# Row sums of the modulation slabs as a high and a low part, the low part by GpSimd

## What is computed

```python
for l in range(DEPTH):
    mod = (silu(c) @ ada_w[l] + ada_b[l])            # 6144 values a layer
    sh1, sc1, g1, sh2, sc2, g2 = split(mod, 6)
    hx = modulate(rms_norm(x, norm_mix_w[l]), sh1, sc1)
    ...
    xq, xdq, xg = split(hx @ w_in[:, :QG_W])         # layer 0: the input projection
    xk, xv, xdk, xdv = split(hx @ w_in[:, QG_W:])    # also of the context rows hc
```

## Time and profile before

| | |
|---|---|
| median of 3 runs | 1220.41 us (1220.31 to 1221.9) |
| the profiled execution | 1222.1 us, of which the span is 1220.2 us |
| PE busy | 1039.8 us (85%) |
| DVE busy | 935.0 us (77%) |
| ACT busy | 605.2 us (50%) |
| POOL busy | 166.7 us (14%) |

### The profile page before, as it was taken

One profiled execution on the slowest core, in us unless ns is written; L12 is line 12 of the kernel. 1 busy time (PEld: TensorE's weight loads), 2 busy tenths in 40 slices (PEclk: granted clock), 3 DMA queues, 4 the chain that ended last, 5 costly groups with the idle time before them and its releaser, 6 DMA issues. The chain is left out here.

```text
span 1220.2 us, 13889 instructions
## 1 busy us (share of the span) xinstructions
PE 1039.8 (85%) x4830; PEld 802.0 (66%) x4830; DVE 935.0 (77%) x1042; ACT 605.2 (50%) x614; POOL 166.7 (14%) x172
## 2 busy tenths in 40 slices
PE   6789999997898983999999999239579999999970
PEld 1576767774565452788888888138558888888860
DVE  5578888964993337799999998273569999999955
ACT  1534222222663122777777776023347777777731
POOL 0100200000100004410000000221063211221005
PEclk9899999997999985999999999659579999999995
DMA  9625798555014024999999997494179999999936
GB/s 372 241 69 211 257 326 311 206 207 224 10 60 129 35 100 136 292 411 413 415 413 414 413 414 312 145 352 140 52 227 392 413 414 415 413 414 414 413 128 229
DMA packets 142861, 334.14 MB, mean 274 GB/s; under 512 B 10848, under 2 KB 12840, under 8 KB 142688
## 3 DMA queue, kind: packets, MB, share of 16 engines
q1 hardware_dynamic: 122936, 279.69, 60.5%
q10 hardware_dynamic: 12392, 28.68, 6.3%
q0 software_dynamic: 7488, 25.19, 5.4%
HBM read 310.42 MB, written 23.15 MB: 273 GB/s over the span
## 5 line engine op out<-in xcount | busy, mean ns | idle before, releaser
L1828 DVE TENSOR_TENSOR w_lo<-ring,w_hi 128x2048 fp32r<-128x2048 f32 x192 | 431.3, 2285 | 25.4 <-ACT w_hi L1674 22.1
L1674 ACT CAST w_hi<-ring 128x2048 fp32r<-128x2048 f32 x192 | 365.8, 1914 | 131.6 <-DMA ring<-in_moe_w_up 50.2
L1919 PE MATMUL bank<-w_hi,xT_hi 128*128 128x512 f32 x512 | 205.2, 401 | 8.1 <-DVE xT_lo L1835 8.1
L1919 PE MATMUL bank<-w_hi,xT_lo 128*128 128x512 f32 x512 | 201.5, 394 | 0.0
L1919 PE MATMUL bank<-w_lo,xT_hi 128*128 128x512 f32 x512 | 201.1, 393 | 0.0
L1368 PE MATMUL bank<-ring_last_parts,arena_parts 128*128 128x512 f32 (+1 forms) x320 | 117.7, 398 | 5.4 <-DVE ring_parts L988 2.7
L1919 PEld LDWEIGHTS bank<-w_hi,xT_hi 128*128 128x128 f32 x512 | 97.3, 190 | 29.4 <-DVE xT_lo L1835 9.8
L1919 PEld LDWEIGHTS bank<-w_hi,xT_lo 128*128 128x128 f32 x512 | 97.1, 190 | 21.2
L1919 PEld LDWEIGHTS bank<-w_lo,xT_hi 128*128 128x128 f32 x512 | 97.5, 190 | 19.4
L1046 DVE SCALAR_TENSOR_TENSOR gate_b<-ring,silu_c,gate_b 128x512 f32<-128x512 f32 x140 | 105.9, 756 | 4.5
L1934 PE MATMUL bank<-w_hi,hT_hi 128*128 128x512 f32 x256 | 101.2, 395 | 7.5 <-DVE w_lo L1828 7.5
(11 more groups left out here) (246 smaller groups left out, 1425.5 us busy)
## 6 DMA issues: line engine op xcount, KB each, us to landing
ring<-in_moe_w_gate SPq DMA_DIRECT2D x64, 1024.0 KB, 11.5
ring<-in_moe_w_up SPq DMA_DIRECT2D x64, 1024.0 KB, 13.4
ring<-in_moe_w_down SPq DMA_DIRECT2D x64, 1024.0 KB, 11.1
ring<-in_ada_w SPq DMA_DIRECT2D x21, 2048.0 KB, 8.7
y_scratch<-shared ACTq DMA_DIRECT2D x32, 512.0 KB, 6.0
ring<-in_w_in ACTq DMA_DIRECT2D x21, 512.0 KB, 3.8
shared<-in_ada_w SPq DMA_DIRECT2D x2, 2048.0 KB, 16.0
x_res<-in_x SPq DMA_DIRECT2D x8, 512.0 KB, 12.4
```

What stands on the lines that cost most here:

```text
L1674: nc.scalar.copy(w_hi[:, buf(u, p), :], half(raw(e, p))).then_inc(s_hi, 3 if isinstance(e, int) and (e, p) == (-1, 3) else 1)
L1828: V.tensor_tensor(w_lo[:, buf(u, p), :], half(raw(e, p)), w_hi[:, buf(u, p), :].bitcast(F32), ALU.subtract).then_inc(s_lo, 3 if isinstance ...
L1919: last = pe.matmul(bank[:, b, :], xs[:, kk, :], ws[:, k, :], start=(kk == 0 and i == 0), stop=(kk == KD - 1 and i == 2))
```

## The change

The sum over partitions of the 18 slabs inside the projection is made from two fp32r parts. ScalarE casts `ada_acc` to a high part (`ada_hi`), one buffer in the first half of `gate1_b`; GpSimd subtracts it from `ada_acc` in place (`ada_lo`); TensorE makes two fp32r matmuls with two columns of ones instead of one fp32 matmul with one. The cast comes five spots after the slab's and the row sum seven, not six. GpSimd takes the low parts in between its decayed keys. As the high part lies where the decay tables were, `decay_exps` moves from spot (6, 1) to (5, 0), ahead of everything else in that spot. The two slabs behind the projection are summed as before.

```diff
+        ada_low = gate2_parts.rearrange("p (b c) -> p b c", b=2)
+        ada_high = gate1_parts[:, 0:HALF]
...
-            rows_after.setdefault(min(spot[nt] + 6, len(spots) - 1), []).append(i)
+            high_after.setdefault(min(spot[nt] + 5, len(spots) - 1), []).append(i)
+            rows_after.setdefault(min(spot[nt] + 7, len(spots) - 1), []).append(i)
...
+                def ada_hi(i):
+
+                    act.wait_ge(m_as, i + 1)
+                    if i >= 1:
+                        act.wait_ge(m_ar, i)
+                    else:
+                        act.wait_ge(m_dk, 1)
+                    nc.scalar.copy(ada_high, ada_acc[:, i % 2, :]).then_inc(m_ahi, 1)
+
...
-                    if (n, t) == (6, 1):
+                    if (n, t) == (5, 0):
                         decay_exps()
+                    for i in high_after.get(p - 1, ()):
+                        ada_hi(i)
                     for r in transposes_after.get(p - 1, ()):
                         copy_qk(r)
...
+                def ada_lo(i):
+
+                    pool.wait_ge(m_ahi, i + 1)
+                    nc.gpsimd.tensor_tensor(ada_low[:, i % 2, :], ada_acc[:, i % 2, :], ada_high.bitcast(F32),
+                                            ALU.subtract).then_inc(m_alo, 1)
+
+                lows = 0
                 for t in range(NK):
                     r = ret_k_units[t]
                     j, c0 = 2, 256
+                    while lows < IN_PROJ and min(spot[slab_spots[lows]] + 5, len(spots) - 1) <= projected(roped_units[r]):
+                        ada_lo(lows)
+                        lows += 1
                     pool.wait_ge(m_rope, r + 1)
...
+                for i in range(lows, IN_PROJ):
+                    ada_lo(i)
...
+                nc.vector.tensor_copy(ones_parts[:], ones[:, 0:2])
...
                 def ada_row_sum(i, b):
-                    pe.wait_ge(m_as, i + 1)
-                    if i >= 1 and i < IN_PROJ:
+                    if i >= IN_PROJ:
+                        pe.wait_ge(m_as, i + 1)
+                        pe.matmul(bank[0:1, b, :], ones[:, 0:1], ada_acc[:, i % 2, :],
+                                  start=True, stop=True).then_inc(m_ar, 1)
+                        return
+                    pe.wait_ge(m_alo, i + 1)
+                    if i >= 1:
                         pe.wait_ge(m_arc, i)
-                    pe.matmul(bank[0:1, b, :], ones[:, 0:1], ada_acc[:, i % 2, :],
-                              start=True, stop=True).then_inc(m_ar, 1)
+                    pe.matmul(bank[0:2, b, :], ones_parts[:], ada_high, start=True, stop=False)
+                    pe.matmul(bank[0:2, b, :], ones_parts[:], ada_low[:, i % 2, :], start=False, stop=True).then_inc(m_ar, 1)
```

More of the change, by code:

```diff
@@ L148, in build_program @@
         norm_a = sb("norm_a", [P, 2, KD])
+        ones_parts = sb("ones_parts", [P, 2], F32R)
+        gate1_parts = parts_of("gate1_parts", D)
         gate1_b = sb("gate1_b", [P, D])
+        gate2_parts = parts_of("gate2_parts", D)
         gate2_b = sb("gate2_b", [P, D])
@@ L507, in build_program @@
         slabs_after = {spot[nt]: i for i, nt in enumerate(slab_spots)}
-        rows_after = {}
+        rows_after, high_after = {}, {}
         for i, nt in enumerate(slab_spots):
-            rows_after.setdefault(min(spot[nt] + 6, len(spots) - 1), []).append(i)
+            high_after.setdefault(min(spot[nt] + 5, len(spots) - 1), []).append(i)
+            rows_after.setdefault(min(spot[nt] + 7, len(spots) - 1), []).append(i)
         roped_units = [u for u, (j, t) in enumerate(units) if any(q[2] in "qk" for q in parts(j, t))]
@@ L539, in build_program @@
         m_as = sem("m_adaln_slab_summed")
+        m_ahi, m_alo = sem("m_adaln_slab_high_part"), sem("m_adaln_slab_low_part")
         m_ar = sem("m_adaln_row")
@@ L844, in _ @@
                         copy_ada_row(i)
+                for i in high_after.get(len(spots) - 1, ()):
+                    ada_hi(i)
                 for i in rows_after.get(len(spots) - 1, ()):
```

## The result

The changed kernel takes 1244.66 us (median of six runs, 1241.22 to 1247.18), the kernel before, run beside it, 1221.16 us (1219.34 to 1222.41). The ratio is 1.0195, 95% interval 1.0181 to 1.0210. The forecast was 1222.3 us, its range 1214 to 1228: "slower" had the largest chance of the three, but the size is missed by 22 us and the range doesn't hold it.

What follows compares the result with a forecast made beforehand. TensorE was taken as the projection's bound, VectorE a close second. The profiled 1222.1 us plus 1.9 at the projection's end gave 1224.0; the runs' median lies 1.7 lower, so 1222.3 us, range 1214 to 1228.

Steps and rivals of the forecast that it cites:

- nothing behind it is changed: Stages after the projection: each starts from the one before, so no loss of their own was counted.
- first stretch: Projection up to 175.45 us, nine of 18 sums: quarter 15 starts 4.0 us late, at 179.4.
- (a): Slab 0, decay exponentials moved to spot (5,0): the sum stalls 0.6 us, which is its saving; nothing left.
- (b): Slab 1's sum after spot (8,1): cast and subtract queue; TensorE 2.4 us late, VectorE 2.1.
- (c): Slabs 2 and 3: subtracts add 0.5 us each, waits before 129.28 absorb 1.0; still 2.1 late.
- (d): Near 142.68 us: slab 4's cast goes ahead of the q and k copy; 0.6 us more, 2.7 late.
- (e): Slabs 4 to 7: subtract delays and slab 8's later load make quarter 15 start 4.0 us late.
- second stretch: Projection after quarter 15: 0.70 us saved on nine sums, 1.1 stalls at slabs 9 and 12; +1.9 at its end.
- My chain of 2.0 us: From slab sum to row sum: 0.6 us cast, 1.2 subtract, 0.1 twice, against one more spot of 1.39.
- rival 1: Projection: VectorE has more room, so TensorE's savings count; -3.6 to -10 us, some 1215; chance 0.25.
- Rival 2: Projection: each subtract keeps VectorE out its whole time, 1.2 us; +7, 1227.5 us; chance 0.18.
- Rival 3: Row sums: fp32r matmuls cost 0.34 us each plus a load; 1224 to 1226 us; chance 0.07.

Runs made afterwards that it cites:

- e6_noshift: Changed kernel with `ones_parts` placed behind the stage's buffers, so the weight ring keeps its old address: 1232.0 us, ratio 1.0093.
- e4_before_sub: Kernel before plus one 128x512 GpSimd subtract per slab, for which no other engine waits at once: 1223.3 us, ratio 1.0023.
- e13_filler: Changed kernel, ring at its old address, plus idle matmuls ahead of four long TensorE waits: 1233.95 us, ratio 1.0115.
- e7_rows8: Changed kernel, ring at its old address, with row sums eight spots after the slab instead of seven: 1230.4 us, ratio 1.0073.
- e8_memset: Changed kernel, ring at its old address, two GpSimd memsets replacing each subtract, low part left out: 1219.6 us, ratio 0.9993.
- e12_pe_only: Changed kernel, ring at its old address, cheap row-sum matmuls on a fixed buffer, no cast or subtract per slab: projection 179.8 us.
- e14_pe_only_filler: e12_pe_only plus ten idle matmuls ahead of TensorE's wait for slab 8: projection 177.6 us.
- e1_pad32: Kernel before plus an unused 32-byte-per-partition tensor ahead of the gate buffers, shifting the ring 32 bytes: 1232.2 us, ratio 1.0098.
- e11_memset3: Changed kernel, ring at its old address, three GpSimd memsets replacing each subtract, low part left out: 1226.3 us, ratio 1.0049.

## Why the prediction was wrong

Counted from quarter 5's low part, VectorE's low parts stand so, in us (before, then e6_noshift):

| | before | e6_noshift | late | forecast late |
|---|---|---|---|---|
| quarter 9 | 25.8 | 25.3 | -0.4 | 0 |
| quarter 10 | 33.1 | 36.2 | 3.1 | 2.1 |
| quarter 12 | 50.0 | 54.1 | 4.1 | 2.1 |
| quarter 15 | 87.6 | 95.1 | 7.5 | 4.0 |
| quarter 20 | 131.7 | 146.2 | 14.5 | about 6 |
| end | 181.5 | 194.2 | 12.7 | 1.9 |

The sum failed at two steps: "nothing behind it is changed" put the experts at 0, and they lose 11.0 us; and the projection was put at +1.9, and loses 12.4 (12.7 in e6_noshift). By the table 3.5 us of the latter miss lie in the first stretch (7.5 late instead of 4.0) and 7.3 in the second, where 2.1 were to be won and 5.2 are lost. The two signs named for being wrong, an early quarter 15 and an early end, both looked to the other side.

**Cost of the parts.** Right for the new sum (0.46 us), for the cast (0.62, I had 0.58) and for the subtract by itself (1.28, I had 1.2).

**The collision was halved.** I took 0.5 us per subtract, from a row with 0.25 us lost beside 256 columns, with 0.9 as the upper bound; it is 1.0 to 1.1 where the two meet in full, beyond that bound, and 0.67 on the mean of all 18 (12.0 us). I misread the nearest row: there GpSimd had itself lost 0.43 us (1.05 instead of 0.62) to the slab instruction before, which ran from 144.03 to 144.77, and VectorE 0.24, together 0.67, about the whole 0.62 of the GpSimd instruction. So 0.25 was what was left of a collision and not its price. The Trainium skill, SBUF — State Buffer, "Who interferes with whom", where VectorE and GpSimd exclude each other for a whole instruction, is nearer to the trace (1.03 to 1.11 us lost beside a subtract of 1.28 alone) than the part of it that I believed. The price alone doesn't make the loss: in e4_before_sub VectorE lost 7.6 us to collisions, and the projection grew by 3.6.

**The first stretch.** Steps (a) and (b) had the right places. The stall at slab 1 is there, as a wait of 2.8 us for ScalarE's copy and 1.1 for GpSimd. Slab 1 made quarter 10 late by 3.1 us, not 2.1, and 1.6 of the 3.1 are the granted clock, as e13_filler shows; step (c) added 1.0, not nothing; steps (d) and (e) added 3.4, not 1.9. I had put quarter 15's start at 179.4 us, and it came at 179.89; that agreement is an accident, since the stage started 3.0 us earlier. It was 7.5 late, not 4.0.

**The second stretch failed.** I had TensorE win 0.70 per sum there, less two stalls. Instead 7.0 us more are lost from quarter 15 to 20 and only 1.8 won behind. Three terms were missing; how the 7.0 us split among them is not shown:

- VectorE's wait for the row sum. I counted who waits for the new chain, and forgot that the slab two further on needs the half that the chain holds: 2.8 us in two waits in the changed kernel, and e7_rows8 shows that it grows to 4.2 when the other wait is relieved. By itself it need not cost: e8_memset has 2.5 us of the same wait and is level with the kernel before.
- The clock. The forecast treated a wait of TensorE as costing its length; at two places, quarter 10 of e6_noshift and slab 8 of e12_pe_only, it is shown to cost 1.6 us beyond it. From 180 to 188 and from 228 to 236 us the changed kernel has 0.81 and 0.79 too, at a price that isn't measured.
- How steep the chain is. It had hardly any room: e8_memset, at 1.1 us in GpSimd, is level with the kernel before; 0.5 us more costs 5.0, of which 2.1 stand at quarter 10, where the clock falls in the one and not in the other. My chain of 2.0 us counted 0.6 over the room once. That each such wait also moves the slab, its load and the next chain is my reading of the rest.

**"TensorE is the bound".** 92.00 busy of 92 us made me call TensorE the bound and rival 1 (up to 12.6 us faster) worth 0.25. e12_pe_only refutes it: with every other cost gone the cheap sum brings 1.7 us, and 3.9 where one fall of the clock is filled (e14_pe_only_filler). VectorE's slabs and their loads set the pace closely behind (TensorE waits 2.44 us for slab 8 itself, and VectorE 2.29 for a load just before), so most of what TensorE is spared turns into waiting.

**The experts.** "Nothing behind it is changed" was the step that missed the other 11 us. The diff allocates `ones_parts` ahead of the ring, and I read that line as 8 bytes and not as an address for everything behind it. e1_pad32 shows the cause, e6_noshift that it is separable.

**The rivals.** Rival 2, the full lock, was nearest in mechanism, but its 7 us were worked out for the projection on the same counting; the projection lost 12.4. Rival 3 (the pair isn't cheap) is refuted by the pitch. Neither would have held the experts' share.

By cause, in the spans: 11.0 us the ring's address; in the projection, against before, cheap sum and chain of 1.1 us together 0 (181.6 against 181.5), half a microsecond more of chain 5.0, and with GpSimd's reads in it 7.6 more. Between the last two the split isn't clean: the subtract also lengthens the chain when it is blocked, and the clock's share lies in both.

No kernel here beats the one before beyond the uncertainty. e8_memset, the best case of the idea, with no reads on GpSimd and the low part left out, is at 0.9993 (0.9980 to 1.0005).

## What to carry to other kernels

A new buffer is a change of address for all that is allocated behind it: put small tensors behind the targets of large loads, and read the DMA rate of stages that the diff doesn't touch. An engine that shows 100% busy is the bound only if its inputs would come earlier too; the cheap test is the gain alone, with its costs left out. Whoever lengthens a chain should list who waits for its end and also who waits for the buffers it holds, and price a stall of TensorE above its length if the granted clock falls behind it. A row taken from a collision shows what one side lost; its price is what both lost together.

## What the hardware showed that I had not expected

- Loads into SBUF ran at 411 to 415 GB/s into a buffer that starts at a multiple of 256 bytes, and at 396 to 401 when it starts 32, 64 or 128 bytes past one, all with the same packets. Over two experts' stretches that is 712 to 715 us against 700 to 703.
- Side by side, a 128x512 GpSimd subtract (1.28 us alone) and VectorE's slab instructions with two SBUF inputs cost VectorE 1.0 to 1.1 us, and GpSimd 0 to 0.5. GpSimd memsets beside the same instructions cost next to nothing (783 ns on the mean for the first of a slab, 1017 with the subtract).
- The granted clock, read over stretches of 8 us, fell behind short waits of TensorE in a stream that is otherwise dense, with a pitch of 0.43 us instead of 0.23: to 0.79 to 0.90 behind waits of 2.8 to 3.6 us in the changed kernel and e6_noshift, to 0.79 behind 2.44 and 0.51 in e12_pe_only, behind 2.54 and 0.96 in e11_memset3 and behind 2.57 in e13_filler, to 0.58 behind 2.73 in e4_before_sub. It stayed at 1.00 behind 2.54 and 0.38 in e8_memset and behind 2.79 alone in e7_rows8. The length of the one wait doesn't tell which it will be.
